# Part of the output projection's products, moved from its own stage into idle slots at the end of the attention stage, with its weights loaded row by row

## The reference, cut to what matters

```python
def even_mixer(x, kv, ...):
    proj = x @ w_in
    q, k, v, u, gate = jnp.split(proj, ...)
    att = moba_prompt(q, k, v)   or   moba_sample(q, k, v, cache_k, cache_v, page_table)
    uc, conv_new = causal_conv(u, conv_buf, conv_w, conv_b)
    h, h_last = rg_lru(uc, h0, w_a, b_a, w_x, b_x, lam)
    rec = h * gelu(gate)
    y = jnp.concatenate([att, rec], axis=-1) @ w_out      # the product concerned ("L2")
x = layer_norm(DN_ALPHA * x + y, g, b)
```

## Time and profile before

| | |
|---|---|
| median of 3 runs | 2494.26 us (2490.69 to 2495.71) |
| the profiled execution's own time | 2493.13 us |
| its span, first to last instruction | 2491.3 us |
| mean granted TensorE clock | 0.939 |
| TensorE matmul busy | 2220.7 us, 89% of the span |
| DVE, ACT, POOL busy | 47%, 34%, 7% |

### The profile page before, as it was taken

One profiled execution on the slowest core, in us unless ns is written; L12 is line 12 of the kernel. 1 busy time (PEld: TensorE's weight loads), 2 busy tenths in 40 slices (PEclk: granted clock), 3 DMA queues, 4 the chain that ended last, 5 costly groups with the idle time before them and its releaser, 6 DMA issues.

```text
span 2491.3 us, 35051 instructions
## 1 busy us (share of the span) xinstructions
PE 2220.7 (89%) x14070; PEld 1970.6 (79%) x14070; DVE 1172.1 (47%) x1622; ACT 851.9 (34%) x1306; POOL 172.7 (7%) x248
## 2 busy tenths in 40 slices
PE   7998889799999979996687898996599999999990
PEld 5776667799999969995576676776599999999990
DVE  1344522433233245665788344003457566666564
ACT  0033411321122133332434132004355555555553
POOL 2011200000000000000233100000100000000001
PEclk9999999899999989997879898997799999999995
DMA  4236762832133012222445211203566766676765
GB/s 137 68 120 190 222 186 96 326 90 89 52 85 104 24 51 68 84 70 81 121 142 180 83 65 51 68 20 98 194 224 223 246 217 231 215 253 210 239 210 174
DMA packets 298953, 349.24 MB, mean 140 GB/s; under 512 B 10952, under 2 KB 253912, under 8 KB 298796
## 3 DMA queue, kind: packets, MB, share of 16 engines
q1 hardware_dynamic: 285574, 299.67, 38.4%
q0 software_dynamic: 12768, 47.49, 5.1%
q10 hardware_dynamic: 504, 0.60, 0.1%
HBM read 299.87 MB, written 47.85 MB: 140 GB/s over the span
## 4 chain that ended last, share of the span: by engine, by line
PE 82%; DVE 8%; ACT 4%; DMA 3%; issue 2%; POOL 1%; SPq 0%; POOLq 0%; DVEq 0%; ACTq 0%
PE ps L815 19%; PE ps L1066 17%; PE ps L1329 10%; PE ps L1311 9%; PE ps L1083 8%; PE ps L1313 6%; PE ps L1314 1%; DMA ring<-cs_rows 1%; PE ps L834 1%; PE ps L829 1%; PE ps L1151 1%; PE ps L917 1%; ACT xT L1388 1%; PE ps L1001 1%; PE ps L1254 1%
## 5 line engine op out<-in xcount | busy, mean ns | idle before, releaser
L815 PE MATMUL ps<-xT,ring 128*128 128x288 f32 (+1 forms) x1184 | 297.1, 414 | 12.3 <-issue 6.5
L815 PEld LDWEIGHTS ps<-xT,ring 128*128 128x128 f32 (+1 forms) x1184 | 225.9, 191 | 81.4 <-issue 9.0
L1311 PE MATMUL ps<-xgs,blk_hi 128*128 128x384 f32 x1232 | 245.8, 338 | 2.8 <-DVE xgs L2309 2.8
L1311 PEld LDWEIGHTS ps<-xgs,blk_hi 128*128 128x128 f32 x1232 | 220.6, 189 | 3.5 <-issue 3.0
L1997 DVE TENSOR_TENSOR fw_l<-ring,fw_h 128x1024 fp32r<-128x1024 f32 (+1 forms) x60 | 79.7, 1331 | 287.9 <-ACT fw_h L1527 287.9
L2304 DVE TENSOR_TENSOR blk_lo<-arena,blk_hi 128x2048 fp32r<-128x2048 f32 (+1 forms) x98 | 197.7, 2025 | 32.7 <-ACT blk_hi L1683 32.7
L1527 ACT ACTIVATE fw_h<-ring 128x1024 fp32r<-128x1024 f32 (+1 forms) x60 | 68.7, 1149 | 399.5 <-PE ps L1066 336.0
L1329 PE MATMUL ps<-blk_hi,hs 128*128 128x512 f32 x704 | 193.6, 393 | 0.0
L1313 PEld LDWEIGHTS ps<-xgs,blk_lo 128*128 128x128 f32 x1408 | 182.4, 192 | 0.0
L1313 PE MATMUL ps<-xgs,blk_lo 128*128 128x192 f32 x1408 | 182.3, 271 | 0.0
L1683 ACT ACTIVATE blk_hi<-arena 128x2048 fp32r<-128x2048 f32 (+1 forms) x98 | 165.7, 1703 | 32.6 <-DMA arena<-in_moe_w 32.5
(11 more groups left out here) (454 smaller groups left out, 3637.0 us busy)
## 6 DMA issues: line engine op xcount, KB each, us to landing
arena<-in_moe_w SPq DMA_DIRECT2D x76, 1024.0 KB, 5.4
ring<-in_moe_w SPq DMA_DIRECT2D x50, 1024.0 KB, 5.4
ring<-in_ssd_w_in SPq DMA_DIRECT2D x48, 512.0 KB, 4.7
ring<-in_ffn_w SPq DMA_DIRECT2D x44, 512.0 KB, 5.2
ring<-in_cache_k SPq DMA_DIRECT2D x64, 256.0 KB, 3.0
arena<-in_cache_v SPq DMA_DIRECT2D x48, 256.0 KB, 3.0
arena<-in_moe_w SPq DMA_DIRECT2D x24, 512.0 KB, 4.1
sorted_x<-ring POOLq DMA_DIRECT2D x1, 10752.0 KB, 33.0
```

The costliest lines, as they stand in the source:

```text
L815: last = mmul(ps[0:M, bank + 2 * j + h, 0:HALF], slot[:, k, j * P:j * P + M], X[:, k0 + k, HALF * h:HALF * (h + 1)], start=(k0 + k == 0), ...
L1311: mmul(o[:, 0:2 * CAP], wh[:, k, :], xgs[:, k, :, :].rearrange("p u n -> p (u n)"), start=(k == 0), stop=False)
```

## The change

The change has five parts:

- `w_l2` is one tile of 8 `k` tiles x 1024 columns. SP loads whole `k` tiles (128 rows of 4 KB each) in the order 4, 5, 6, 7, 0, 1, 2, 3, two to a semaphore.
- A new TensorE function `l2_half(d, ks, start, stop)` makes the products of column tile `d` over the given `k` tiles. For `d` = 0 and `k` = 4, 6, 0, 2 it first waits for the weights.
- In the attention loop, after `weighted(15)` (`s` = 17), the recurrent half (`k` 4 to 7) of tiles `d` = 0 and 1 is computed; after `weighted_s(3)` (`s` = 18), that of `d` = 2. Their sums stay open in banks 0/1, 4/5 and 6/7.
- To free those banks the key transposes go to bank 6 in place of 4, and the cached-key scores to banks 4 and 5 in place of 5 and 6.
- After the loop TensorE waits for the last copy into `cat` (`out_up`) itself, finishes `d` = 0 to 2 with `k` 0 to 3, and makes `d` = 3 to 7 whole. DVE adds the residual per two tiles as before, from the new banks.

```diff
-        w_l2 = [at(18688 + 2048 * n, KD, CW) for n in range(4)]
+        w_l2 = at(18688, KD, D)
...
+        def l2_bank(d):
+
+            b = (0, 4, 6, 2)[d % 4]
+            return ps[:, b:b + 2, 0:HALF]
+
+        L2_K = (4, 6, 0, 2)
...
             sp.wait_ge(out_mm, OUTS["pv_s", NR - 2] + 1)
-            for j in range(KD // 2):
-                for dst, src in pair(w, 0, KD, j * CW)(w_l2[j]):
-                    sp.dma_start(dst, src).then_inc(loaded[(C_L2 + j) % SLOTS], 16)
+            for n, k0 in enumerate(L2_K):
+                for k in (k0, k0 + 1):
+                    sp.dma_start(w_l2[:, k, :], w[k * P:(k + 1) * P, :]).then_inc(loaded[(C_L2 + n) % SLOTS], 16)
...
+            def l2_half(d, ks, start, stop):
+
+                o = l2_bank(d)
+                for k in ks:
+                    if d == 0 and k in L2_K:
+                        c = C_L2 + L2_K.index(k)
+                        pe.wait_ge(loaded[c % SLOTS], 32 * (c // SLOTS + 1))
+                    for h in range(2):
+                        last = mmul(o[:, h, :], w_l2[:, k, d * P:(d + 1) * P], cat[:, k, HALF * h:HALF * (h + 1)],
+                                    start=(start and k == ks[0]), stop=(stop and k == ks[-1]))
+                if stop and d % 2:
+                    last.then_inc(used, 1)
...
                 if 2 <= s < NA + 2:
                     weighted(s - 2)
+                if s == NA + 1:
+                    pe.wait_ge(ex_ok, NA)
+                    l2_half(0, range(4, 8), True, False)
+                    pe.wait_ge(s_raw, 2 * NR)
+                    l2_half(1, range(4, 8), True, False)
...
                 if pr is not None:
                     weighted_s(pr)
+                    if pr == NR - 1:
+                        pe.wait_ge(kt_act, 2 * NA)
+                        pe.wait_ge(kt_dve, 2 * NA)
+                        l2_half(2, range(4, 8), True, False)
...
-            for j in range(KD // 2):
-                unit("l2", j, 4 * (j % 2), [part_l2(j)], cat)
+            pe.wait_ge(out_up, len(OUTS))
+            for d in range(KD):
+                if d >= 4 and d % 2 == 0:
+                    pe.wait_ge(free["l2"], d // 2 - 1)
+                if d >= 3:
+                    l2_half(d, range(4, 8), True, False)
+                l2_half(d, range(4), False, True)
             layer_norm(0)
...
-            dve.wait_ge(out_up, len(OUTS))
-            dve.sem_inc(free["l2"], 2)
             for j in range(KD // 2):
-                residual("l2", j, 4 * (j % 2), ln_ready if j == 3 else None)
+                dve.wait_ge(used, done("l2", j))
+                for d in (2 * j, 2 * j + 1):
+                    i = stt(halves(xT[:, d, :]), halves(xT[:, d, :]), ALPHA, l2_bank(d), ALU.mult, ALU.add)
+                i.then_inc(ln_ready if j == 3 else free["l2"], 1)
```

More of the change, by code:

```diff
@@ L916, in keys @@
                 for pg in range(QUAD):
-                    last = tr(ps[:, 7 if t % 2 else 4, pg * P:(pg + 1) * P], k_pages[s % 4][:, pg, t * P:(t + 1) * P], ident[:])
+                    last = tr(ps[:, 7 if t % 2 else 6, pg * P:(pg + 1) * P], k_pages[s % 4][:, pg, t * P:(t + 1) * P], ident[:])
                 last.then_inc(kt_mm, 1)
@@ L964, in quad_scores @@
                 for t in range(AT):
-                    last = mmul(ps[32 * t:32 * t + 32, 5 + half, :], qa[t][:, pr, b2, :], kt[n % 2][:, t, :], start=(b2 == 0), stop=(b2 == 1))
+                    last = mmul(ps[32 * t:32 * t + 32, 4 + half, :], qa[t][:, pr, b2, :], kt[n % 2][:, t, :], start=(b2 == 0), stop=(b2 == 1))
                 last.then_inc(qs_mm, 1)
@@ L1041, in _ @@
                     weighted_s(pr)
-            def part_l2(j):
-                c = C_L2 + j
-                return (loaded[c % SLOTS], 32 * (c // SLOTS + 1), w_l2[j], 0, KD)
-            for j in range(KD // 2):
-                unit("l2", j, 4 * (j % 2), [part_l2(j)], cat)
+                    if pr == NR - 1:
[9 more added lines that the diff above has]
+                l2_half(d, range(4), False, True)
             layer_norm(0)
@@ L1440, in keys_out @@
                 act.wait_ge(kt_mm, 4 * s + t + 1)
-                f(kt[s % 2][:, t, :], ps[:, 4, :], ACT.Copy).then_inc(kt_act, 1)
+                f(kt[s % 2][:, t, :], ps[:, 6, :], ACT.Copy).then_inc(kt_act, 1)
             def turned(s):
@@ L1473, in raw_out @@
                 act.wait_ge(qs_mm, 4 * pr + 2 * half + 2)
-                f(p_s[pr % 2][:, 512 * half:512 * half + 512], ps[:, 5 + half, :], ACT.Copy).then_inc(s_raw, 1)
+                f(p_s[pr % 2][:, 512 * half:512 * half + 512], ps[:, 4 + half, :], ACT.Copy).then_inc(s_raw, 1)
                 if half:
```

## The result

Over 20 runs each, the changed kernel takes 2484.28 us (2478.96 to 2489.35), the kernel before 2490.93 (2482.14 to 2495.71): ratio 0.9972, 95% interval 0.9963 to 0.9982, 6.65 us faster by the medians. The profiled execution has a span of 2486.5 us, against 2491.3; its own time, 2489.35 us, is the longest of the changed kernel's 20.

A forecast was written before the change was run, and what follows sets the result against it. TensorE was taken to bound the kernel, busy 89% of the span. Terms -11.7 + 3.2 + 3.4 - 2.7 = -7.8 us took 2493.13 to 2485.3, plus 1.13 to the median: 2486.5 us, range 2484.0 to 2491.5.

The forecast's parts named there:

- step 2: Tiles 0 and 1 in TensorE's idle hole after `weighted(15)`: late weight landings delay the last pair's transposes by 3.2 us.
- the last step of the sum: From the profiled execution's own time to the median of the runs: 1.13 us added to 2485.3, giving 2486.5 us.
- Step 1: L2 loses the recurrent half of three column tiles, 48 records: -11.7 us.
- Step 3: Filling the hole keeps TensorE's clock at its upper level through the last pair's transposes and weighted sums: -2.7 us.
- rival A: The clock still falls, later, taking in the weighted sums: gain 6.2 us, or 5.1 with the transposes too; chance 0.20.
- Step 4: Tile 2 between weighted sums and transposes back: +3.4 us on the path, worth only the 0.46 us wait for ACT's copy.
- Steps 5 and 6: Changed waits and banks cost nothing, bounds -0.1 and +0.2 us; SP's later loads arrive in time, so L2's gain stays.
- Rival C: Products wait for weights at a low clock and hold the transposes: 0.7 to 1.7 us slower, 2495.0 to 2496.0; chance 0.06.

The follow-up runs named there:

- column pieces: The changed kernel with weights loaded in pieces of 4 k tiles x 256 columns, recurrent half of tiles 0 to 3 first: ratio 0.9965, stretch 72.84 us.
- early rows: The changed kernel with the recurrent half's four row loads issued before the last eight value pages, run twice: ratios 0.9946 and 0.9949, stretches 75.28 and 73.52 us.
- the filled kernel: The kernel before with 11 unread products after `weighted(15)`, L2 whole, run twice: ratios 0.9967 and 0.9966, stretch 78.41 us both times.

## Why the prediction was right or wrong

**The size of the change was right.** Forecast -7.8 us; the stretch gives -7.1 (and 6.9 by the second trace), the medians -6.65 with an interval from 4.5 to 9.2.

**The failed steps are the baseline and its scatter, and, inside the sum, step 2.** The absolute time was too high by 2.2 us (2486.5 against 2484.28), and what failed there is the last step of the sum, "with the 1.13 us to the median". The median of three runs, 2494.26, was taken for the kernel's own. With 20 runs it is 2490.93: the profiled execution, 2493.13, lay 2.2 above the median and not 1.1 below it. 2490.93 - 7.8 would have been 2483.1. The same three runs gave "This kernel's runs differ by 0.2%, 5.0 us", from which the chance of 0.74 for a change clear of that was drawn. The 20 runs of before spread over 13.6 us and those of the changed kernel over 10.4, and the interval of the change begins at 4.5 us, inside the 5.0. So the medians show that the kernel is faster, but not surely by more than the scatter that the prediction had named.

**Step 1, products out of L2:** right. 208 records in 50.72 us, forecast 50.7.

**Step 2, the landing:** the mechanism was right, the term mis-sized. The delay of the transposes was 3.81 us, forecast 3.2, and that 0.6 is nearly all of what separates -7.1 from -7.8. The fourth row landed at 339.5 in before's time, not 339.0: the third landed at 337.8, in before's time 336.8 and earlier than the 337.5 of the forecast, and the fourth 2.7 us behind it, where the prediction had used x_prompt's mean step of 1.47. It took the DMAs to land one after the other at even steps; the fourth and the fifth landed 0.3 us apart. The loads ran at 407 and 416 GB/s. That does not agree with the Trainium skill, "DMA: Bandwidth & Descriptors", section Where 436 GB/s comes from, which has about 358 as the limit of loads from HBM. That a smaller price was open in the same step, two column pieces in place of four rows, was not seen; it is 1.0 us, in one trace of each.

**Step 3, the clock:** right, and shown apart from the products: 2.5 us, forecast 2.7 (2.62 in the changed kernel). The single last transpose takes 0.31 us at the upper level and not pair 2's 0.24. But it isn't safe. In two traces of the kernel with early rows the low level took in the sums, as rival A had it; in both traces of the changed kernel it did not.

**Step 4, tile 2:** right. From the end of the sums to the closed block it is 3.34 us longer, forecast 3.4; tile 2 alone is worth 0.5 us, forecast 0.46.

**Steps 5 and 6:** the waits and the other banks cost nothing that the stretch shows. The gain was carried on: the first SwiGLU products behind the layer norm start 6.15 us earlier in the trace (442.00 against 448.15), L2's end likewise (409.54 against 415.69).

**Rival C** did not happen, but its mechanism was one line away: with the recurrent half loaded last the ratio is 0.9991 (0.9979 to 1.0002).

## What to carry to other kernels

Work put into an idle slot of an in-order queue is worth the idle time that it fills and the clock that it keeps, not the work that it takes out elsewhere: 17 products cut to the slots gained 10.75 us in the stretch, 24 not cut to them 7.1. A part of that is the earlier loading, since early rows without the cutting gained 5.7 and 7.4. Load first what the slot needs, in the shape in which the fewest DMAs release it. And measure such a change on its own stretch of the trace: single runs of the kernel before differ by up to 13.6 us, and the filled kernel's median fell by 6.5 us where its stretch fell by 2.5.

## What was not expected of the hardware

Eleven products that nobody reads made the kernel faster, by 2.5 us in the stretch, since the work behind them ran at 2.4 GHz and not at 1.2. After 8 us of unbroken work the clock still fell in one trace with early rows, behind pauses of less than 0.8 us each, and stayed up in the trace with column pieces, behind the same work and the same pauses. So what TensorE does in this stretch does not settle alone where the clock falls. Much of the scatter between executions goes with it: behind L2 they spend 275 to 300 us at 1.2 GHz.
